# Four first up units in the banks of the down product, and down products 0 and 1 both behind round 3

## The chip, the core and the metric

The kernel is one program for one core of a Trainium2 chip. The core has a matrix engine (TensorE, PE), a vector engine (VectorE, DVE), a scalar engine (ScalarE, ACT), a general one (GpSimd, POOL) and a queue that here issues nearly all loads (SyncE, SP). Each engine works through its own list of instructions in order and waits on semaphores that the others raise. The metric is the time of the whole program on the device in microseconds (us), the median of several runs.

## What is computed

Two transformer-like blocks follow each other on 256 tokens of width 1024, in float32. The part that the change touches is the feed-forward net (FFN) of the first block, of width 2816:

```python
def conv_ffn(h, w_up, taps, conv_b, w_down, rows):
    a, g = jnp.split(h @ w_up, 2, axis=-1)
    bsz, t, f = g.shape
    ...
        g2, tp = g.reshape(bsz, rows, GRID_W, f), taps
    gc = lax.conv_general_dilated(g2, tp[:, :, None, :].astype(g.dtype), (1, 1), 'SAME',
                                  dimension_numbers=('NHWC', 'HWIO', 'NHWC'), feature_group_count=f)
    gc = gc.reshape(bsz, t, f) + conv_b
    return (a * jax.nn.gelu(gc, approximate=False)) @ w_down
...
        h2 = modulate(rmsnorm(x, norm_ffn[l]), sh2, sc2)
        x = x + g2 * conv_ffn(h2, w_up[l], conv_w[l], conv_b[l], w_down[l], rows)
```

The factor `g2` ahead of the product is one of six vectors of `silu(c) @ w_ada`; its four blocks of weights (ada20 to ada23) are still worked off during this FFN.

## The kernel before

**Weights.** All weights come from HBM in chunks of 1 MB, in the one order of the list `CHUNKS`. SP loads chunk n into place n % 3 of the ring `raw` (`RING = 3`, load at L510) as soon as chunk n-3 has been used up: a product chunk when DVE has split it (semaphore `w_lo`), an ada chunk when DVE has folded it (`ada_late`). A product chunk is split in two halves of the value: ACT writes the high part `whi` (`split_hi`, L595), DVE the low part `wlo` (`split_lo`, L604); both have three places as well, and a place is free when PE has done the product three chunks (ada ones not counted) earlier (`multiplied`). Every product is then three matmuls (L1140 to L1142): high by high, high by low, low by high.

**The FFN in rounds.** `for j in range(FFT // 2)` runs 11 rounds on each engine. Round j has two up products, `fg{j}` (the branch that is convolved) and `fa{j}` (the other), each of 48 matmuls into one PSUM bank, and a down product `fd{j}`, also of 48 matmuls, which adds into banks 4 to 7 over all rounds. On PE a round is `gemm(fg{j})`, `gemm(fa{j})` and, from round 2 on, `down(j - 2)` (L1484 to L1490). The up units lie in banks 0 and 1 in turn (all fg in one, all fa in the other) and wait until the unit two earlier is emptied; one exception was there already: fa1 goes to bank 6, and fa2 then waits for fa0.

ACT in round j: copies fg{j} out of its bank in four steps (L834, L835), splits two chunks (whi), waits for the convolution, gelu (L848), from round 2 on a third split, then `uhi`, the high part of the round's result (L854). DVE in round j: four of the eight outer taps for both halves (L2191, 8 instructions), a split (wlo), the other four taps, a split, the product with fa{j} (L2205), from round 2 on a third split, then `ulo` (L2212). The chunk that is split is always the third after the one just multiplied. In rounds 1, 3, 5 and 7 an ada chunk is worked on as well: ACT scales it in two halves (L823), DVE folds it at the end of the round (L2218 to L2220), and this frees its place in `raw`.

What sets the order around the change is written out by hand: the list of chunks (`ffn_chunks`, `ADA_AT`), the lists of the three engines and the banks in `g_bank` and `g_open`. Around it, the order of chunks before is fg2, ada20, fa2, fd0, fg3, fa3, fd1, fg4, ada21, fa4, fd2, fg5.

## Time and profile before

| | us |
|---|---|
| median of 3 runs | 1023.29 |
| lowest, highest run | 1022.83, 1025.29 |
| the profiled execution | 1022.01 |
| its span, first to last instruction | 1020.2 |
| PE busy in the span | 964.4 (95%) |
| DVE busy, ACT busy | 744.3 (73%), 501.6 (49%) |

The trace is of one execution; times in it count from the start of the span. The rounds of the FFN run from about 237 to 441 us. In the rows, a duration includes the tail of an instruction that the next one already overlaps, so the step from one start to the next is the better measure of what an instruction takes in a row. "issue" marks idle time for which the profile finds no releaser.

### The profile page before, as it was taken

How to read it: one execution, taken by the hardware profiler on the slowest of the kernel's cores; microseconds unless marked ns; L12 is line 12 of the kernel's file. 1: busy time of each engine (PE TensorE's matmuls, PEld its weight loads, DVE VectorE, ACT ScalarE, POOL GpSimd, SP SyncE). 2: the span in 40 equal slices, each digit the busy share in tenths (PEclk: the TensorE clock that was granted, in tenths of full speed). 3: DMA queues.
4: the chain of work that ended last, by engine and by line, in shares of the span. 5: the costliest groups of instructions: out<-in, count | busy, mean ns of one | idle time of the engine just before them, and what ended most of it. 6: DMA issues, size and time to landing. Idle time of an engine off the chain costs nothing.

```text
span 1020.2 us, 17808 instructions
## 1 busy us (share of the span) xinstructions
PE 964.4 (95%) x7576; PEld 904.6 (89%) x7576; DVE 744.3 (73%) x1083; ACT 501.6 (49%) x623; POOL 16.7 (2%) x35
## 2 busy tenths in 40 slices
PE   5999999899989999989998989989999999999997
PEld 3578999898989999988997989989989999999986
DVE  5879988878888798847977966644595776666664
ACT  5644344625464464427754544324543554545463
POOL 0000000002000000000100000000000000000000
PEclk9999999999989999979999999999999999999999
DMA  9997353364366557654756875735653455555541
GB/s 339 284 294 257 115 166 125 124 207 143 114 226 214 193 173 247 174 116 83 145 122 152 139 151 172 123 97 118 143 180 129 145 192 180 195 178 195 176 165 42
DMA packets 142719, 171.76 MB, mean 168 GB/s; under 512 B 3241, under 2 KB 129473, under 8 KB 142641
## 3 DMA queue, kind: packets, MB, share of 16 engines
q1 hardware_dynamic: 140352, 165.63, 55.7%
q0 software_dynamic: 1088, 2.57, 0.7%
q10 hardware_dynamic: 1200, 2.43, 0.7%
q8 instruction: 60, 0.98, 0.4%
q14 instruction: 19, 0.15, 0.0%
HBM read 169.55 MB, written 1.06 MB: 167 GB/s over the span
## 4 chain that ended last, share of the span: by engine, by line
PE 59%; DVE 10%; ACT 4%; issue 3%; DMA 2%; DVEq 0%; ACTq 0%
PE bank L1140 18%; PE bank L1142 17%; PE bank L1141 17%; DVE wlo L604 3%; ACT whi L595 2%; PE bank L1678 2%; DMA raw<-in_w_in_dram 1%; DVE arena L2326 1%; DVE arena L2191 1%; PE bank L1619 1%; DVE arena L2287 1%; DVE arena L1865 1%; DMA raw<-in_w_up_dram 1%; ACT arena L953 0%; PE bank L1455 0%
## 5 line engine op out<-in xcount | busy, mean ns | idle before, releaser
L1140 PE MATMUL bank<-hhi,whi 128*128 128x256 f32 (+1 forms) x1744 | 512.6, 294 | 23.7 <-issue 8.0
L1141 PE MATMUL bank<-hlo,whi 128*128 128x256 f32 (+1 forms) x1744 | 505.4, 290 | 0.0
L1142 PE MATMUL bank<-hhi,wlo 128*128 128x256 f32 (+1 forms) x1744 | 505.3, 290 | 0.0
L604 DVE TENSOR_TENSOR wlo<-raw,whi 128x2048 fp32r<-128x2048 f32 x131 | 299.7, 2290 | 151.2 <-ACT whi L595 110.7
L1140 PEld LDWEIGHTS bank<-hhi,whi 128*128 128x128 f32 x1744 | 339.7, 195 | 33.2 <-issue 21.1
L1141 PEld LDWEIGHTS bank<-hlo,whi 128*128 128x128 f32 x1744 | 340.0, 195 | 4.1 <-issue 1.2
L1142 PEld LDWEIGHTS bank<-hhi,wlo 128*128 128x128 f32 x1744 | 339.6, 195 | 2.5
L595 ACT ACTIVATE whi<-raw 128x2048 fp32r<-128x2048 f32 x131 | 250.5, 1912 | 119.6 <-PE bank L1142 69.1
L1140 PE MATMUL bank<-whi,hhi 128*128 128x256 f32 (+1 forms) x256 | 88.2, 344 | 0.8 <-ACT arena L1102 0.8
L1141 PE MATMUL bank<-wlo,hhi 128*128 128x256 f32 (+1 forms) x256 | 86.7, 339 | 0.0
L1142 PE MATMUL bank<-whi,hlo 128*128 128x256 f32 (+1 forms) x256 | 86.6, 338 | 0.0
L2191 DVE SCALAR_TENSOR_TENSOR arena<-arena,params 128x256 f32<-128x256 f32 x176 | 71.6, 479 | 6.5 <-ACT arena L835 6.5
L2581 DVE SCALAR_TENSOR_TENSOR arena<-bank,params,arena 128x255 f32<-128x255 f32 (+1 forms) x88 | 36.4, 476 | 31.5 <-ACT arena L1050 31.2
L1140 PEld LDWEIGHTS bank<-whi,hhi 128*128 128x128 f32 x256 | 49.2, 192 | 6.7 <-ACT arena L1102 1.2
L1142 PEld LDWEIGHTS bank<-whi,hlo 128*128 128x128 f32 x256 | 49.2, 192 | 5.1
L1141 PEld LDWEIGHTS bank<-wlo,hhi 128*128 128x128 f32 x256 | 49.3, 193 | 4.8 <-issue 0.2
L946 ACT ACTIVATE arena<-bank 128x512 f32<-128x512 f32 x18 | 10.8, 598 | 77.0 <-PE bank L1142 77.0
L1050 ACT ACTIVATE arena<-bank,params 128x256 f32<-128x256 f32 x44 | 18.5, 470 | 61.1 <-PE bank L1142 61.1
L806 ACT ACTIVATE arena<-XT 128x512 f32<-128x512 f32 x12 | 7.6, 631 | 44.9 <-DVE XT L2155 28.3
L1956 DVE SCALAR_TENSOR_TENSOR raw<-raw,small 128x256 f32<-128x256 f32 x72 | 29.5, 478 | 0.0
L1678 PE MATMUL bank<-arena 64*64 64x64 f32 x512 | 18.6, 220 | 2.9 <-issue 2.9
L1678 PEld LDWEIGHTS bank<-arena 64*64 64x64 f32 x512 | 16.9, 135 | 4.6 <-issue 3.0
(351 smaller groups left out, 866.9 us busy)
## 6 DMA issues: line engine op xcount, KB each, us to landing
raw<-in_w_in_dram SPq DMA_DIRECT2D x46, 1024.0 KB, 8.4
raw<-in_w_up_dram SPq DMA_DIRECT2D x44, 1024.0 KB, 5.1
raw<-in_w_down_dram SPq DMA_DIRECT2D x22, 1024.0 KB, 5.0
raw<-in_w_ada_dram SPq DMA_DIRECT2D x19, 1024.0 KB, 5.3
raw<-in_w_branch_dram SPq DMA_DIRECT2D x6, 1024.0 KB, 5.4
arena<-in_w_ada_dram SPq DMA_DIRECT2D x10, 512.0 KB, 9.3
raw<-in_w_out_dram SPq DMA_DIRECT2D x4, 1024.0 KB, 5.0
raw<-in_w_o_dram SPq DMA_DIRECT2D x4, 1024.0 KB, 5.1
```

The lines of the kernel that those rows point to most:

```text
L595: act.activation(whi[:, g % RING, :], raw[:, n % RING, :], ACT.Copy).then_inc(w_hi, 1)
L604: dve.tensor_tensor(wlo[:, g % RING, :], raw[:, n % RING, :], whi[:, g % RING, :].bitcast(F32), ALU.subtract).then_inc(w_lo, 1)
L946: act.activation(dst, two(g_bank(u)), func).then_inc(g_empty["act"], 1)
L1050: ins = act.activation(acc2[:, b, n, t, :], g_bank(f"s{w}{j}")[:, T * t:T * (t + 1)], ACT.Copy, scale=col)
L1140: pe.matmul(o, wh, ah, start=start, stop=False, **kw)
L1141: pe.matmul(o, wh, al, start=False, stop=False, **kw)
L1142: return pe.matmul(o, wl, ah, start=False, stop=stop, **kw)
L1619: ins = pe.matmul(o[:, P * h:P * (h + 1)], lhsT(c, h), rhs(c, h), start=True, stop=True)
L1678: ins = pe.matmul(o[m, 64 * h:64 * h + 64], lhsT[k, 4 * c + h, m] if lhsT is ANT else lhsT[k, 4 * c + h, :], rhs[k, 4 * c + h, :], start=T ...
L1956: ins = dve.scalar_tensor_tensor(out=w[:, k % 2, :], in0=w[:, k, :], scalar=silu_c[:, k, 0:1], in1=w[:, k % 2, :], op0=ALU.mult, op1=ALU.add)
L2191: ins = dve.scalar_tensor_tensor(out=a, in0=pad[:, b, t, dy:dy + 4, dx:dx + 64], scalar=par("conv_w", k=FFT * tap + 2 * j + t), in1=a, op0 ...
L2581: ins = dve.scalar_tensor_tensor(out=acc2[:, b, n, t, d:T], in0=ps[:, T * t:T * (t + 1) - d], scalar=par("ffn_conv", k=2 * FFT * (2 - d) + ...
```

## The change

The order of loads, the banks and the order of work in rounds 2 and 3 change together. The lines that only drop a condition which is always true are left out of the diff.

- `downs(tag, j)` says which down products follow round j: none after round 2, both 0 and 1 after round 3, the others as before. The list of chunks, the PE's list and the splits on ACT and DVE use it. The order of chunks becomes fg2, ada20, fa2, fg3, fa3, fd0, fd1, fg4, ada21, fa4, fd2, fg5.
- fg1, fa1, fg2, fa2 go to banks 4 to 7, which the down product doesn't use until down 0, and wait for no bank. fg3 and fa3 wait for fg0 and fa0, the last users of their banks. PE waits ahead of down 0 until fg2 and fa2 are emptied.
- Round 2 has two splits on ACT and DVE instead of three, round 3 has four instead of three. On ACT the first half of ada21's scaling moves behind the second split of round 3.

```diff
+    def downs(tag, j):
+        if tag == "f" and j in (2, 3):
+            return [(), (0, 1)][j - 2]
+        return (j - 2,) if j > 1 else ()
...
-            if j > 1:
-                chunk(f"{tag}d{j - 2}", rows(down, 2 * (j - 2)), (2, D))
+            for d in downs(tag, j):
+                chunk(f"{tag}d{d}", rows(down, 2 * d), (2, D))
...
+        FILL_BANK = {"fg1": 4, "fa1": 5, "fg2": 6, "fa2": 7}
+        FILL_AFTER = {"fg1": None, "fa1": None, "fg2": None, "fa2": None, "fg3": "fg0", "fa3": "fa0"}
...
-            return bank[6] if u == "fa1" else bank[g_banks[g_no(u) % 2]]
+            return bank[FILL_BANK.get(u, g_banks[g_no(u) % 2])]
...
-                if j + 1 in ADA_AT:
+                if j + 1 in ADA_AT and j != 3:
                     ada_scale(ADA_AT[j + 1], 0)
...
+                if j == 3:
+                    ada_scale(ADA_AT[j + 1], 0)
+                for d in downs("f", j)[:-1]:
+                    split_hi(act, G[f"fd{d}"] + RING)
...
-                if j > 1:
-                    split_hi(act, G[f"fd{j - 2}"] + RING)
+                for d in downs("f", j)[-1:]:
+                    split_hi(act, G[f"fd{d}"] + RING)
...
-                before = {"fa1": None, "fa2": g_no("fa0")}.get(u, n - 2)
-                if n >= 2 and before is not None:
-                    e, k = g_emptied(before)
+                if u in FILL_AFTER:
+                    if FILL_AFTER[u]:
+                        pe.wait_ge(*g_done(FILL_AFTER[u]))
+                elif n >= 2:
+                    e, k = g_emptied(n - 2)
                     pe.wait_ge(g_empty[e], k)
...
-                if j == 2:
-                    pe.wait_ge(*g_done("fa1"))
-                if j > 1:
-                    down(j - 2)
+                if j == 3:
+                    pe.wait_ge(*g_done("fg2"))
+                    pe.wait_ge(*g_done("fa2"))
+                for d in downs("f", j):
+                    down(d)
...
+                for d in downs("f", j)[:-1]:
+                    split_lo(dve, G[f"fd{d}"] + RING)
...
-                if j > 1:
-                    split_lo(dve, G[f"fd{j - 2}"] + RING)
+                for d in downs("f", j)[-1:]:
+                    split_lo(dve, G[f"fd{d}"] + RING)
```

Where it moves instructions, the first place is the load queue between the load of fg2 and that of fg5. Before, from the load of fg2 on (w_up is an fg or fa chunk, w_down an fd chunk, w_ada an ada chunk; the wait is for the chunk three earlier):

```order
43 L510 DMA raw<-in_w_up_dram 128x8x256 [waits w_lo] x2
44 L510 DMA raw<-in_w_ada_dram 128x8x256 [waits w_lo]
45 L510 DMA raw<-in_w_up_dram 128x8x256 [waits w_lo]
46 L510 DMA raw<-in_w_down_dram 128x2x1024 [waits w_lo]
47 L510 DMA raw<-in_w_up_dram 128x8x256 [waits ada_late]
48 L510 DMA raw<-in_w_up_dram 128x8x256 [waits w_lo]
49 L510 DMA raw<-in_w_down_dram 128x2x1024 [waits w_lo]
50 L510 DMA raw<-in_w_up_dram 128x8x256 [waits w_lo]
```

And the same place after the change:

```order
43 L519 DMA raw<-in_w_up_dram 128x8x256 [waits w_lo] x2
44 L519 DMA raw<-in_w_ada_dram 128x8x256 [waits w_lo]
45 L519 DMA raw<-in_w_up_dram 128x8x256 [waits w_lo] x2
46 L519 DMA raw<-in_w_up_dram 128x8x256 [waits ada_late]
47 L519 DMA raw<-in_w_down_dram 128x2x1024 [waits w_lo] x2
48 L519 DMA raw<-in_w_up_dram 128x8x256 [waits w_lo]
```

The load that waits for the fold of ada20 was that of fg3 and is now that of fa3; the two w_down loads stand together behind it.

The second place is DVE's list in round 3, from its first taps to the fold of ada21. Before (the three wlo are those of fg4, fa4 and fd2):

```order
261 L2191 SCALAR_TENSOR_TENSOR arena<-arena,params 128x256 [waits dve_step] x6
262 L604 TENSOR_TENSOR wlo<-raw,whi 128x2048 [waits g_full,w_hi,raw_loaded2]
263 L2191 SCALAR_TENSOR_TENSOR arena<-arena,params 128x256 [waits dve_step] x8
264 L604 TENSOR_TENSOR wlo<-raw,whi 128x2048 [waits g_full,w_hi,raw_loaded1]
265 L2205 TENSOR_TENSOR arena<-bank,arena 128x512 [waits g_full,u_hi,gelu_out]
266 L604 TENSOR_TENSOR wlo<-raw,whi 128x2048 [waits down_used,w_hi,raw_loaded2]
267 L2212 TENSOR_TENSOR hlo<-arena,hhi 128x512 [waits down_used,u_hi]
268 L2218 TENSOR_TENSOR raw<-raw 128x1024 [waits ada_scaled]
```

After the change (the four wlo are those of fd1, fg4, fa4 and fd2):

```order
260 L2205 SCALAR_TENSOR_TENSOR arena<-arena,params 128x256 [waits dve_step] x6
261 L613 TENSOR_TENSOR wlo<-raw,whi 128x2048 [waits g_full,w_hi,raw_loaded1]
262 L2205 SCALAR_TENSOR_TENSOR arena<-arena,params 128x256 [waits dve_step] x8
263 L613 TENSOR_TENSOR wlo<-raw,whi 128x2048 [waits g_full,w_hi,raw_loaded2]
264 L613 TENSOR_TENSOR wlo<-raw,whi 128x2048 [waits down_used,w_hi,raw_loaded1]
265 L2220 TENSOR_TENSOR arena<-bank,arena 128x512 [waits g_full,u_hi,gelu_out]
266 L613 TENSOR_TENSOR wlo<-raw,whi 128x2048 [waits down_used,w_hi,raw_loaded2]
267 L2227 TENSOR_TENSOR hlo<-arena,hhi 128x512 [waits down_used,u_hi]
268 L2233 TENSOR_TENSOR raw<-raw 128x1024 [waits ada_scaled]
```

The split of fd1 has come in ahead of fg4's, which moved from between the two halves of the taps to behind them; the split of fa4 now waits for a down product.

## Rows read from the trace of the kernel before

**Rows 1.** The page: span, and busy time of each engine.
```profile
span 1020.2 us, 17808 instructions
PE 964.4 (95%) x7576; PEld 904.6 (89%) x7576; DVE 744.3 (73%) x1083; ACT 501.6 (49%) x623; POOL 16.7 (2%) x35
```

**Rows 2.** PE's waits: line, releaser, us in total, times, longest.
```profile
PE bank L1140 <- issue: 8.0, 4, 5.8
```

**Rows 3.** PE's timeline: start, us, engine, line, instruction, [idle before <- releaser].
```profile
284.15 0.55 PE L1140 MATMUL bank<-hhi,whi 128*128 128x256 f32 x1 [5.78 <-issue]
...
321.32 0.36 PE L1140 MATMUL bank<-hhi,whi 128*128 128x256 f32 x1 [0.46 <-issue]
...
357.19 0.36 PE L1140 MATMUL bank<-hhi,whi 128*128 128x256 f32 x1 [0.84 <-issue]
```

**Rows 4.** The chain that ended last, in time: start, us, what.
```profile
274.57 5.17 DMA raw<-in_w_up_dram
279.76 1.92 ACT whi L595
281.68 2.47 issue
...
284.71 0.21 PE bank L1141
...
289.42 0.12 PE bank L1142
```

**Rows 5.** The load queue's timeline: start and us of the issue.
```profile
274.57 1.00 SPq L510 DMA_DIRECT2D raw<-in_w_up_dram  x2
...
299.27 0.37 SPq L510 DMA_DIRECT2D raw<-in_w_down_dram  x1
311.31 0.99 SPq L510 DMA_DIRECT2D raw<-in_w_up_dram  x2
```

**Rows 6.** DVE's timeline, rounds 2 to 4.
```profile
289.94 2.28 DVE L604 TENSOR_TENSOR wlo<-raw,whi 128x2048 fp32r<-128x2048 f32 x1
...
293.79 3.25 DVE L2191 SCALAR_TENSOR_TENSOR arena<-arena,params 128x256 f32<-128x256 f32 x8 [0.96 <-ACT arena L835]
296.96 2.29 DVE L604 TENSOR_TENSOR wlo<-raw,whi 128x2048 fp32r<-128x2048 f32 x1
299.16 3.26 DVE L2191 SCALAR_TENSOR_TENSOR arena<-arena,params 128x256 f32<-128x256 f32 x8
302.32 2.29 DVE L604 TENSOR_TENSOR wlo<-raw,whi 128x2048 fp32r<-128x2048 f32 x1
...
306.07 2.29 DVE L604 TENSOR_TENSOR wlo<-raw,whi 128x2048 fp32r<-128x2048 f32 x1 [0.85 <-issue]
...
310.86 0.42 DVE L2220 TENSOR_TENSOR arena<-raw 128x256 f32<-128x256 f32 x1
...
318.93 2.29 DVE L604 TENSOR_TENSOR wlo<-raw,whi 128x2048 fp32r<-128x2048 f32 x1 [4.48 <-issue]
```

**Rows 7.** ACT's timeline, rounds 2 and 3.
```profile
290.06 0.63 ACT L854 ACTIVATE hhi<-arena 128x512 fp32r<-128x512 f32 x1 [0.37 <-DVE arena L2205]
292.18 0.39 ACT L834 ACTIVATE arena<-bank 128x256 f32<-128x256 f32 x1 [1.49 <-PE bank L1142]
...
304.06 1.92 ACT L595 ACTIVATE whi<-raw 128x2048 fp32r<-128x2048 f32 x1 [0.98 <-DMA raw<-in_w_down_dram]
```

**Rows 8.** Stretches behind waits: busy times, then PEclk; and two matmuls that end one.
```profile
284.20:288.30 4.10, 4.10 (x19) 4.10 (x20) 4.10 (x9) 1.52 (x3) 0.00 (x0) 0.50 0.83 269
201.40:204.40 3.00, 3.00 (x26) 3.00 (x27) 2.90 (x7) 1.26 (x2) 0.00 (x0) 1.00 0.00 0
482.60:485.60 3.00, 3.00 (x18) 3.00 (x17) 2.93 (x4) 2.99 (x5) 0.00 (x0) 0.58 0.04 9
...
482.33 0.36 PE L1140 MATMUL bank<-hhi,whi 128*128 128x256 f32 x1 [2.07 <-DVE arena L2287]
201.30 0.36 PE L1140 MATMUL bank<-hhi,whi 128*128 128x256 f32 x1 [2.72 <-ACT whi L595]
```

More of the change, by code:

```diff
@@ L838, in _ @@
                 ins.then_inc(g_empty["act"], 1)
-                if G[f"fg{j}"] + RING < N_SPLIT:
-                    split_hi(act, G[f"fg{j}"] + RING)
-                if j + 1 in ADA_AT:
+                split_hi(act, G[f"fg{j}"] + RING)
+                if j + 1 in ADA_AT and j != 3:
                     ada_scale(ADA_AT[j + 1], 0)
-                if G[f"fa{j}"] + RING < N_SPLIT:
-                    split_hi(act, G[f"fa{j}"] + RING)
+                split_hi(act, G[f"fa{j}"] + RING)
+                if j == 3:
+                    ada_scale(ADA_AT[j + 1], 0)
+                for d in downs("f", j)[:-1]:
+                    split_hi(act, G[f"fd{d}"] + RING)
                 if j + 1 in ADA_AT:
@@ L2198, in _ @@
                 ins.then_inc(conv_out, 1)
-                if G[f"fa{j}"] + RING < N_SPLIT:
-                    split_lo(dve, G[f"fa{j}"] + RING)
+                split_lo(dve, G[f"fa{j}"] + RING)
+                for d in downs("f", j)[:-1]:
+                    split_lo(dve, G[f"fd{d}"] + RING)
                 dve.wait_ge(gelu_out, j + 1)
```

## The prediction, made before the changed kernel ran

> **What bounds the kernel now.** I read four views in this order. First the page: TensorE (PE) is busy for 95% of the span [rows 1], so only time in which PE stands still can be won, and any new standstill is a loss. Second, the waits of PE: the largest sum is 8.0 us in 4 waits, the longest 5.8 us [rows 2]. PE's timeline places all four inside the first feed-forward part: 5.78 us before the matmul at 284.15, then 0.46, 0.84 and 0.90 us before those at 321.32, 357.19 and 393.13, of which three stand in [rows 3]. By their order these are the first matmuls of fg3, fg5, fg7 and fg9. Third, the chain of work shows what the long wait was for [rows 4]: a load of w_up issued at 274.57 lands 5.17 us later, ScalarE (ACT) makes whi for 1.92 us, VectorE (DVE) makes wlo in the 2.47 us called issue, PE goes on at 284.15. Fourth, the load queue: the load at 274.57 was issued right after DVE had folded ada20, since ada20 held the ring place that this load needs [rows 5]. So PE doesn't wait for a bank here; it waits for a place in the raw ring.
>
> From PE's next wait I read the same loop: fold of ada21 ends at 310.86 + 0.42 = 311.28, loads go out at 311.31, wlo of fg5 runs from 318.93 to 321.22, PE starts at 321.32 [rows 3, 5, 6]. PE was ready at 320.86. The slack of this loop is therefore below zero by 0.46 us: whatever delays the fold of ada21 delays PE by as much.
>
> **The change, part by part.**
>
> *Banks.* PE's first standstill in the rounds is the one before 284.15 [rows 2, 3]; up to the end of fa2 it never waits for a bank, so four units in other banks remove nothing there. For fg3 the bank wait falls away as well, but in the old order its weights were last, not its bank. Price 0, covered by the weights that come later.
>
> *The first standstill.* The new order of chunks is fg2, ada20, fa2, fg3, fa3, fd0, fd1. Loads look three chunks back: now fg3 takes the place of fg2 (early) and fa3 takes that of ada20. ACT and DVE in round 1 have the same number of splits as before, one of them of fg3 in place of fd0, so ada20 is folded at the same time and the load goes out at 274.57 again, now for fa3. PE does fg3 where it did down 0: both are 48 matmuls, 0.12 us apart [rows 4], 5.76 us. It comes to the end of fg3 at 278.4 and waits until 284.15 for fa3. Same work done, same wait, same slow matmuls behind it: 0 us.
>
> *Round 3 on DVE.* Here the sum is made. DVE splits in round 2 only two chunks (fa3, fd0) where it had three; the split at 289.94 [rows 6] goes. So ACT writes uhi at 290.06 as before [rows 7], can copy fg3 out straight after it (fg3 is long finished), 0.6 us later by the 0.63 of that row, and DVE starts 1.6 us behind the first of the four copies (292.18 to 293.79). The taps of round 3 start at about 290.06 + 0.6 + 1.6 = 292.2 and not at 293.79 [rows 6]: 1.6 us early.
> Against that stands the place of fg4's split. It was the first of the round: taps from 293.79, wlo from 296.96 to 299.25, and at 299.27 the load of fd2 went out into its ring place [rows 5, 6]. Now the first split is fd1's and fg4's comes after the second half of the taps: one wlo (299.16 - 296.96 = 2.20) and eight taps (302.32 - 299.16 = 3.17 by the start of the next row) later, 5.4 us. fg4's split then ends at 292.2 + 3.17 + 2.20 + 3.17 + 2.29 = 303.0, and the load of fd2 goes out 3.8 us later than before.
> From there to the fold I take the old distance: load at 299.27, whi at 304.06 which waited 0.98 us for that load, wlo at 306.07, ulo, fold to 311.28 [rows 5 to 7], 12.0 us. Nothing new comes between: wlo of fa4, whose load goes out when fd1 is split at 297.6 and lands at about 302.8 (5.2 after, as in [rows 4]), ends at about 307.1, ahead of the 307.8 at which fd2 lands; and down 1, for which fd2's place in whi must wait, ends at 303.6 as before. So ada21 is folded at 315.0, fg5's weights are ready 3.8 us later, and PE starts fg5 at about 325.1. PE itself has done the same six units by 320.9, so this standstill grows from 0.46 to 4.2 us. **Term: +3.8 us.**
>
> Bounds of it. Above: the whole 5.4 us, if ACT's early copy brings nothing. Below: 5.4 - 1.6 - 0.8 = 3.0, if DVE's 0.85 us of idleness before 306.07 [rows 6] takes up part; I take 3.8, because in the new order that idleness grows (DVE is free at 307.7 and waits for fd2 till 309.8) and hides nothing.
>
> *The clock.* After the 5.78 us wait, the stretch from 284.20 has a granted clock of 0.50, the 1.2 GHz level, and 19 matmuls in 4.1 us. After a wait of 2.07 us before 482.33 the stretch behind shows 0.58; after one of 2.72 us before 201.30 it shows 1.00 [rows 8]. A new wait of 4.2 us lies between them and I expect a fall: 15 matmuls at 0.213 instead of 0.12 us (the steps at 1.2 GHz and at the full level), 1.4 us. Of this PE gets back what it waits before fg7 anyway, 0.84 us [rows 3], as the loads of the next rounds hang on DVE and hardly on PE. **Term: +0.5 us**, from 0 (no fall) to 1.4 (nothing given back).
> By the Trainium skill (TensorE: Matmul & The Clock Gate, Loop structure matters more than you think) a wait for a DMA between matmuls lets PE go cold, whereas a copy out of PSUM does not; the trace agrees for the wait at 284.15, and 1.4 us would be the price here too.
>
> *Smaller things.* The new waits of PE before down 0 (banks of fg2 and fa2 emptied) are met at 290.0, when DVE has multiplied fa2; PE comes there at 292.1: 0. Behind that wait stand down 0 and down 1. Margins get thin: fd1's split ends at 297.7, PE wants it at 297.9; fg4's ends at 303.0, PE wants it at 303.6. Price 0, to 0.5 us if I err by half a microsecond. The end of round 3 moves scaling of ada21 on ACT behind one split; both halves end before 306.5, no one waits.
>
> *After fg5.* From there order and work are the old ones. Both old idle times (0.84, 0.90) stay, since DVE, ACT and loads form a loop of their own. The rest of the span is PE's: the shift of the FFN's end goes to the end.
>
> **Sum** against the profiled execution: 1022.01 + 3.8 + 0.5 = 1026.3 (its span 1020.2 would be 1024.5). That execution is 1.3 us below the median of 1023.29; on the median's scale the forecast is 1027.5 us, with own bounds of 1023.29 + 3.0 = 1026.3 and 1023.29 + 5.4 + 0.5 = 1029.2.
>
> **Rivals.**
> *B, the bank was the limit (faster).* Were the wait before 284.15 one for a bank, the fill would close it: -5.8 us and -1.8 for the 19 or 20 slow matmuls, less what the loads then still hold back: 1023.3 - 7.6 = 1015.7 us. It decides from the moment that fa3's weights are there before 278.4. For it speaks only that the trace names no releaser (issue) at 284.15. Against it: the chain through load, whi and wlo ends 0.1 us before the matmul [rows 4, 6]. In this case I give it 0.06.
> The Trainium skill (Perfetto Trace Analysis, Optimizing Tensor Performance, Matmuls) says that matmul groups should rotate through different PSUM banks so that one's copy out overlaps the next's matmuls; that is this rival, and the trace speaks against it in this stretch, as the load is what comes last.
> *C, part is given back (same).* If the loads after fg5 were paced by PE, the waits of 0.84 and 0.90 us would vanish once PE is late: 4.3 - 1.7 = 2.6, 1025.9 us; the same reading holds if DVE gains a little more than 1.6 us in round 3. Against it: DVE's rows from 318.93 on follow each other without PE in between. 0.20.
> *D, the thin margins break (slower still).* PE waits also for fd1's and fg4's splits and the full clock loss stays: +5.4 + 1.4 = +6.8, less nothing: 1030.1 us. It decides if wlo of fd1 ends later than 297.9. 0.12.
> *A, as forecast*: 0.62.
>
> **How the numbers follow.** A measurement of this kernel tells about 0.3% (3.1 us) from no change. Slower by more: D and nearly nine tenths of A, 0.12 + 0.55 = 0.67. Within: C and the rest of A, 0.27. Faster: B, 0.06. The range takes in A, C and most of D and leaves room below C, where the two terms of round 3 would cancel further: 1023.4 to 1029.8 us.
>
> **What would show it.** In the new profile: PE's wait of 5.8 us again, but before fa3, at about 284.1; DVE's taps of round 3 at about 292.2; the load of fd2 issued at about 303.0; the fold of ada21 ending at about 315; PE's wait before fg5 of about 4.2 us with a granted clock near 0.5 after it; later waits of 0.3 to 0.9 us as before. Wrong I would be if the first wait is gone or much shorter (B), or if the wait before fg5 is under 2 us.

## The result, and the profile after

The changed kernel took 1028.5 us (median of 7 runs, 1025.8 to 1031.4) where the kernel before, run beside it, took 1022.8 us (7 runs, 1016.0 to 1025.3). The ratio of the means of the two sets is 1.0069, with an interval of 1.0038 to 1.0100: slower, by 7.1 us of 1022.8 (the medians alone are 5.7 us apart). On the scale of the 1023.29 us before, that is 1030.3 us, just above the top of the range I gave (1029.8), and 2.8 us above the forecast. The interval reaches into the range, so the miss of the range by itself is thin; that the loss is larger than forecast is shown below by the traces and by a second set of runs. The sign was right, the size too small.

The page of the changed kernel, which answers to [rows 1]:

```profile
span 1026.7 us, 17809 instructions
PE 959.8 (93%) x7576; PEld 899.4 (88%) x7576; DVE 744.7 (73%) x1083; ACT 501.2 (49%) x623; POOL 16.7 (2%) x35
```

No matmul came or went (7576 in both). PE's busy time is 4.6 us less than before; that says little, since the same kernel was busy for 965.7 us in its second trace (e1). What can be compared are the waits. PE's timeline of the changed kernel, with the four waits that answer to [rows 3] (start, us, idle before it and what released it):

```profile
285.72 0.55 PE L1153 MATMUL bank<-hhi,whi 128*128 128x256 f32 x1 [5.73 <-issue]
...
329.10 0.55 PE L1153 MATMUL bank<-hhi,whi 128*128 128x256 f32 x1 [6.22 <-issue]
...
365.63 0.36 PE L1153 MATMUL bank<-hhi,whi 128*128 128x256 f32 x1 [0.44 <-issue]
...
401.51 0.36 PE L1153 MATMUL bank<-hhi,whi 128*128 128x256 f32 x1 [0.83 <-issue]
```

The line numbers are 9 to 15 higher than before: L1153 is the old L1140, L613 the old L604, L519 the old L510. The waits stand before fa3, fg5, fg7 and fg9. The first is as long as it was (5.73 against 5.78 us), only a unit later. The second has grown from 0.46 to 6.22 us. Together they are 13.2 us, where they were 8.0 [rows 2]: +5.2 us.

**One offset first.** The first matmul of fg0 starts at 239.15 us in this trace and at 237.55 in that of before, in code that the change doesn't touch. PE's granted clock shows it; the same stretch of both kernels, first after, then before (PE busy time and matmuls, PEld, DVE, ACT, POOL, then PEclk):

```profile
204.00:211.00 7.00, 7.00 (x54) 7.00 (x54) 2.32 (x2) 0.00 (x0) 0.00 (x0) 0.87 0.46 150
```

```profile
204.00:211.00 7.00, 7.00 (x61) 7.00 (x60) 3.05 (x4) 0.00 (x0) 0.00 (x0) 1.00 0.46 149
```

A granted clock of 0.87 leaves 54 matmuls in 7 us, one of 1.00 leaves 61. In e1, which is the changed kernel once more, the clock of that stretch was full, so the fall belongs to the execution, not to the change. Below I therefore measure from the first matmul of fg0. To where PE starts on the sums behind the first FFN it is 204.2 us before and 210.9 us after: **+6.8 us**. What follows the FFN is within 2 us of before (576.6 against 578.5 us). So the loss lies in the FFN, as forecast.

**Where it arises.** The loads of the changed kernel answer to [rows 5]:

```profile
304.60 0.37 SPq L519 DMA_DIRECT2D raw<-in_w_down_dram  x1
317.89 0.99 SPq L519 DMA_DIRECT2D raw<-in_w_up_dram  x2
```

and DVE's timeline to [rows 6]:

```profile
293.74 3.25 DVE L2205 SCALAR_TENSOR_TENSOR arena<-arena,params 128x256 f32<-128x256 f32 x8 [0.76 <-ACT arena L844]
296.92 2.28 DVE L613 TENSOR_TENSOR wlo<-raw,whi 128x2048 fp32r<-128x2048 f32 x1
299.12 3.25 DVE L2205 SCALAR_TENSOR_TENSOR arena<-arena,params 128x256 f32<-128x256 f32 x8
302.29 2.28 DVE L613 TENSOR_TENSOR wlo<-raw,whi 128x2048 fp32r<-128x2048 f32 x1
...
312.65 2.29 DVE L613 TENSOR_TENSOR wlo<-raw,whi 128x2048 fp32r<-128x2048 f32 x1 [3.35 <-issue]
...
317.44 0.42 DVE L2235 TENSOR_TENSOR arena<-raw 128x256 f32<-128x256 f32 x1
...
326.71 2.29 DVE L613 TENSOR_TENSOR wlo<-raw,whi 128x2048 fp32r<-128x2048 f32 x1 [5.68 <-issue]
```

The taps of round 3 start at 293.74 (forecast 292.2, with the offset of 1.6: 293.8). fg4's split, now behind the second half of the taps, starts at 302.29, and the load of fd2 goes out at 304.60 (forecast 303.0 + 1.6 = 304.6). Up to here the forecast holds to a tenth. Then two steps are longer than the same steps before. ACT's timeline of the changed kernel has the moments at which the two loads are used:

```profile
310.64 1.92 ACT L604 ACTIVATE whi<-raw 128x2048 fp32r<-128x2048 f32 x1 [2.20 <-DMA raw<-in_w_down_dram]
324.71 1.91 ACT L604 ACTIVATE whi<-raw 128x2048 fp32r<-128x2048 f32 x1 [10.19 <-DMA raw<-in_w_up_dram]
```

From issue to use, fd2's load takes 310.64 - 304.60 = 6.04 us (before: 304.06 - 299.27 = 4.79), and that of fg5 324.71 - 317.89 = 6.82 us (before: 5.61). Each is 1.2 us longer, and both lie on the loop that ends in fg5's weights. fg5 thus comes 329.10 - 239.15 = 89.95 us after fg0, 6.2 us later than before (321.32 - 237.55 = 83.77), where I had 3.8. The stretch behind fg5 brings the other 0.6 us.

**What differs in the two loads.** In the profile's list of DMA queues there is, besides the queue of the loads, one called "instruction", which now and then moves a single packet of 0.02 MB. The DMA page of two windows of half a microsecond in the changed kernel, 306.0 to 306.5 and 321.0 to 321.5, one in either load (queue, packets, MB, share of the 16 engines):

```profile
q8 instruction: 1, 0.02, 13.1%
```

```profile
q1 hardware_dynamic: 187, 0.19, 107.5%
q8 instruction: 1, 0.02, 13.7%
```

Before, no such packet lay in fg5's load. The same view of that kernel, 311.3 to 317 (the last line gives both loads issued then, and the median to landing):

```profile
q1 hardware_dynamic: 1470, 1.49, 80.1%
issues: line engine op xcount, KB each, median us to landing
raw<-in_w_up_dram SPq DMA_DIRECT2D x2, 1024.0 KB, 6.9
```

But one lay in another load of that kernel, that of fg4, issued at 284.08. Two windows of its DMA view, 284 to 285 and 286.5 to 287.5, have the time from issue to landing and the packet:

```profile
raw<-in_w_up_dram SPq DMA_DIRECT2D x1, 1024.0 KB, 6.5
```

```profile
q8 instruction: 1, 0.02, 6.7%
```

Whether these packets lengthen the loads, or only lie there, is what e7 and e9 ask.

### The profile page after: what moved, and what is told of

The parts are those of the page before. It is cut to its first block, busy times and chain, and to the rows that moved or that the text cites. A ratio compares the mean times of both kernels' runs of the same rounds, so it can differ in the third digit from the quotient of the medians.

```text
span 1026.7 us, 17809 instructions
## 1 busy us (share of the span) xinstructions
PE 959.8 (93%) x7576; PEld 899.4 (88%) x7576; DVE 744.7 (73%) x1083; ACT 501.2 (49%) x623; POOL 16.7 (2%) x35
## 4 chain that ended last, share of the span: by engine, by line
PE 53%; DVE 13%; ACT 4%; issue 4%; DMA 4%; DVEq 0%; ACTq 0%
PE bank L1153 16%; PE bank L1154 16%; PE bank L1155 16%; DVE wlo L613 4%; DVE arena L2205 2%; PE bank L1692 2%; DMA raw<-in_w_in_dram 2%; ACT whi L604 2%; DMA raw<-in_w_up_dram 1%; DVE arena L2341 1%; DVE arena L2302 1%; DVE arena L2371 1%; DMA raw<-in_w_down_dram 1%; DVE arena L1879 1%; PE bank L1633 1%
## 5 line engine op out<-in xcount | busy, mean ns | idle before, releaser
L1153 PE MATMUL bank<-hhi,whi 128*128 128x256 f32 (+1 forms) x1744 | 512.3, 294 | 30.0 <-issue 13.6
L613 DVE TENSOR_TENSOR wlo<-raw,whi 128x2048 fp32r<-128x2048 f32 x131 | 299.8, 2290 | 154.4 <-ACT whi L604 107.5
L1153 PEld LDWEIGHTS bank<-hhi,whi 128*128 128x128 f32 x1744 | 339.2, 195 | 39.4 <-issue 27.3
L604 ACT ACTIVATE whi<-raw 128x2048 fp32r<-128x2048 f32 x131 | 250.4, 1912 | 130.9 <-PE bank L1155 68.5
L1153 PE MATMUL bank<-whi,hhi 128*128 128x256 f32 (+1 forms) x256 | 87.9, 344 | 0.8 <-ACT arena L1113 0.8
L1153 PEld LDWEIGHTS bank<-whi,hhi 128*128 128x128 f32 x256 | 49.0, 191 | 6.7 <-ACT arena L1113 1.2
```

Of the source, the lines that this page charges most:

```text
L604: act.activation(whi[:, g % RING, :], raw[:, n % RING, :], ACT.Copy).then_inc(w_hi, 1)
L613: dve.tensor_tensor(wlo[:, g % RING, :], raw[:, n % RING, :], whi[:, g % RING, :].bitcast(F32), ALU.subtract).then_inc(w_lo, 1)
L1153: pe.matmul(o, wh, ah, start=start, stop=False, **kw)
```

## The experiments

All ratios are against the kernel before, run on the same chip in the same call; its medians there were 1021.3, 1021.4, 1022.1 and 1021.0 us. The number that I compare beside the time is the length of the FFN in each trace, from fg0's first matmul to the sums behind it: 204.2 us before, 210.9 us after. A load is timed in two ways: to its use, as above, and to its landing, the moment when all of it has arrived, which can be earlier when ACT is still busy.

### The change again, and its parts

**e1** is the changed kernel, with nothing edited.

> The changed kernel once more, to see which parts of its loss come back. In its first trace PE waited 5.73 us before fa3 and 6.22 us before fg5, the load of fd2 took 6.0 us from issue to use and that of fg5 6.8 us (4.8 and 5.6 in the trace of the kernel before), and PE was already 1.6 us late at the first round. Theory 1 (the place of fg4's split on VectorE makes the loop longer by 3.8 us, the slower loads and the 1.6 us are chance): wait before fg5 between 4.0 and 6.5 us, loads between 4.8 and 6.8 us, the 1.6 us gone or back as the clock falls; time 4 to 7 us above the kernel before. Theory 2 (the new order of loads makes these two loads slower each time): both loads again 6.0 and 6.8 us, wait before fg5 again 6.2 us.

Measured: 1028.8 us (1026.9 to 1032.2), ratio 1.0077 (1.0052 to 1.0102); FFN 211.6 us. PE's timeline has 5.75 us before fa3 and, before fg5:

```profile
328.00 0.55 PE L1153 MATMUL bank<-hhi,whi 128*128 128x256 f32 x1 [6.42 <-issue]
```

The two loads took 5.80 and 6.95 us, again with an instruction packet in each. So neither the 6.2 us nor the longer loads were chance. The clock behind fg5's wait was at 0.50 here, where the first trace had 0.66, and from fg5 on this trace loses 1.4 us, not 0.6.

**e5** keeps the changed order of the work but takes the banks of before, so that PE has to wait for them:

```
-        FILL_BANK = {"fg1": 4, "fa1": 5, "fg2": 6, "fa2": 7}
-        FILL_AFTER = {"fg1": None, "fa1": None, "fg2": None, "fa2": None, "fg3": "fg0", "fa3": "fa0"}
+        FILL_BANK = {"fa1": 6}
+        FILL_AFTER = {"fa1": None, "fa2": "fa0"}
```

> The changed kernel with the banks and bank waits of the kernel before; order of loads, splits and PE's units stay as changed. Now fa3 must wait until fa2 is emptied, so PE's wait before fa3 should grow from 5.7 to about 11.5 us. Theory 1 (behind round 3 the loop of loads and splits sets the time, not PE): the wait before fg5 shrinks by the same 5.8 us to about 0.5, later parts and the time stay within 1.5 us of the changed kernel. Rival (PE sets the time there): the 5.8 us add up, 5 to 6 us slower than the changed kernel.

Measured: 1026.4 us, ratio 1.0060 (1.0039 to 1.0080); FFN 210.3 us. One of the ten executions took 5215 us and isn't in the ratio. By the ratios this is 1.7 us below e1, a little over the 1.5 us expected, and within the intervals. PE's timeline:

```profile
290.71 0.56 PE L1153 MATMUL bank<-hhi,whi 128*128 128x256 f32 x1 [11.02 <-DVE arena L2220]
...
328.20 0.36 PE L1153 MATMUL bank<-hhi,whi 128*128 128x256 f32 x1 [0.37 <-issue]
```

PE waits 11.02 us for a bank before fa3 and comes out 6 us later than with the new banks (290.71, in e1 284.72), and yet fg5 starts at the same time (328.20, in e1 328.00) and the FFN is no longer. The changed order makes the loss with the old banks too.

It would be too much to read from this that PE's place in the rounds doesn't matter, for two things cancel. PE's lateness does reach the loop: ACT's splits in round 3 now wait for PE. ACT's timeline has the split of fd2, 2.2 us behind the landing of its load:

```profile
310.65 1.92 ACT L604 ACTIVATE whi<-raw 128x2048 fp32r<-128x2048 f32 x1 [1.73 <-PE bank L1155]
```

Against that both loads are short: fd2's lands after 4.91 us and fg5's after 5.88, where the two traces of the changed kernel have 6.02 and 5.78, and 6.80 and 6.93. PE's instructions come later here, and no instruction packet lies in either load.

**e6** does the other part alone: the order of before, with fg1 and fa1 in the banks 4 and 5.

```
-            return bank[6] if u == "fa1" else bank[g_banks[g_no(u) % 2]]
+            return bank[{"fg1": 4, "fa1": 5}.get(u, g_banks[g_no(u) % 2])]
...
-                before = {"fa1": None, "fa2": g_no("fa0")}.get(u, n - 2)
+                before = {"fg1": None, "fa1": None, "fg2": g_no("fg0"), "fa2": g_no("fa0")}.get(u, n - 2)
```

> The kernel before with fg1 and fa1 in banks 4 and 5 and no bank wait for fg1, fa1; fg2 and fa2 wait for fg0 and fa0. Orders unchanged. Theory 1: no unit waited for its bank there, so PE's waits are 5.8, 0.5, 0.8 and 0.9 us as before and the time is within 0.2% of the kernel before. Rival (banks cost something in the first rounds): 1 to 3 us faster and a shorter wait before fg3.

Measured: 1020.6 us, ratio 1.000 (0.998 to 1.002); FFN 203.5 us, and PE still waits 5.76 us in the first place. Banks alone bring nothing and cost nothing.

**e2** gives round 3 of the changed kernel the three splits that it had before, of fg4 and fa4 in the old places and of fd2 last, and has fd1 split in round 2:

```
+                up3 = ("fg4", "fa4") if j == 3 else (None, None)
+                split_hi(act, G[up3[0]] if up3[0] else G[f"fg{j}"] + RING)
...
-                for d in downs("f", j)[-1:]:
-                    split_hi(act, G[f"fd{d}"] + RING)
+                if j > 1:
+                    split_hi(act, G[{2: "fd1", 3: "fd2"}[j]] if j < 4 else G[f"fd{j - 2}"] + RING)
```

and the same on DVE. The first half of ada21's scaling goes back to its old place too.

> The changed kernel, but with the split of fd1 back in round 2 on ScalarE and VectorE, so that rounds 2 and 3 have three splits each and fg4's split stands between the two halves of the taps again; banks, order of loads and order on PE stay as changed. Theory 1 (the split's place on VectorE is the loss): the load of fd2 goes out 4 to 5 us earlier against the first round, PE waits under 1 us before fg5, time 4 to 7 us below the changed kernel and within 2 us of the kernel before. Theory 2 (order and speed of loads are the loss): the wait before fg5 shrinks by at most 3.8 us and 2.4 us of it stay; time 2 us or more above the kernel before. In both the wait of 5.7 us before fa3 stays, as it hangs on the fold of ada20.

Measured: 1017.3 us (1015.2 to 1021.5), ratio 0.9960 (0.9943 to 0.9977); FFN 203.4 us. In its trace the load of fd2 goes out at 299.32, the fold of ada21 ends at 312.4, fg5's load takes 5.30 us, and PE has no wait before fg5. So it is the place of the splits, fg4's behind the taps above all, that the loss hangs on: with it undone, the whole 6.8 us and a little more are gone, although the banks, the two down products together and the order of the weights on PE are the changed kernel's. This run doesn't tell the parts of the loss from each other, as both loads are short here too (to landing 4.74 and 5.27 us). It is 11.5 us below e1, where I expected 4 to 7. The time is below that of before by 4 us, of which the FFN shows 0.8 and the part behind it 2.0 in the one trace; I can't place more of it.

### What the loop is worth

If the ring place behind a fold is what holds PE up, an earlier fold must shorten both waits. **e3** is the kernel before, with the fold of the ada chunk (three additions) moved from the end of the round to right behind the second half of the taps:

```
                 ins.then_inc(conv_out, 1)
+                if j + 1 in ADA_AT:
+                    c = ADA_AT[j + 1]
+                    dve.wait_ge(ada_scaled, 2 * (c - 19))
+                    w = raw[:, ada_place[c] % RING, :].rearrange("p (k n) -> p k n", k=KT)
...
+                    dve.tensor_tensor(acc_late[:, c % 4, :], w[:, 0, :], w[:, 1, :], ALU.add).then_inc(ada_late, 1)
```

> The kernel before with one edit: VectorE folds the ada chunk right behind the second half of the taps instead of at the end of the round, so its ring place comes free 4 to 6 us earlier. If PE's long wait is for a ring place (my reading): the wait of 5.8 us before fg3 shrinks to about 2 us, those before fg5, fg7 and fg9 vanish, fewer slow matmuls; 5 to 8 us faster than before. If it is for a bank or for the load path itself: wait and time unchanged.

Measured: 1012.1 us (1009.7 to 1014.7), ratio 0.9909 (0.9885 to 0.9933); FFN 195.6 us, 8.6 less than before. Its load queue and PE (two views):

```profile
271.46 0.99 SPq L510 DMA_DIRECT2D raw<-in_w_up_dram  x2
```

```profile
274.30 0.39 PE L1140 MATMUL bank<-hhi,whi 128*128 128x256 f32 x1 [0.58 <-DVE arena L2212]
...
281.96 0.35 PE L1140 MATMUL bank<-hhi,whi 128*128 128x256 f32 x1 [1.65 <-ACT whi L595]
```

The load that stood at 274.57 [rows 5] goes out 3.1 us earlier, 4.2 us when both are counted from fg0 (at 238.65 here). The gain is a little more than the 5 to 8 us expected. PE's waits in the FFN come to 2.2 us, where they were 8.0, and the three later ones are gone; since PE now waits 1.65 us and not 5.78, its clock also stays at the full level behind it (1.00 from 281.96 to 285), where before it was at 0.50 [rows 8].

**e4** puts both together, the early fold and the changed kernel with the three splits of e2.

> The changed kernel with three splits each in rounds 2 and 3 and with the early fold. If the new order has a gain that only the ring hid, it is faster than the kernel before with the early fold by what PE still waits there; by the ring theory both orders do the same work ahead of the same load, so the two come out within 1 us of each other, 5 to 8 us faster than the kernel before, with a wait of about 2.5 us before fa3.

Measured: 1012.3 us (1008.9 to 1014.4), ratio 0.9908 (0.9883 to 0.9934); FFN 196.8 us. PE's timeline, and two stretches behind the wait:

```profile
283.31 0.36 PE L1150 MATMUL bank<-hhi,whi 128*128 128x256 f32 x1 [2.23 <-ACT whi L604]
```

```profile
283.40:286.40 3.00, 3.00 (x19) 3.00 (x20) 3.00 (x9) 0.00 (x0) 0.00 (x0) 0.70 0.69 223
286.40:289.00 2.60, 2.60 (x18) 2.60 (x17) 2.60 (x2) 2.44 (x2) 0.00 (x0) 0.69 0.45 149
```

Once the fold is early, the new banks and the new order add nothing to it: e3 and e4 are the same within their intervals. PE waits 2.23 us in one place, and behind that its granted clock is 0.70.

**e8 and e10** fill that wait of e4 with idle products (they go into a free bank and are overwritten), to ask what the clock costs: 14 products in e8, 4 in e10.

```
+                if j == 3:
+                    pe.wait_ge(*g_done("fg1"))
+                    keep_clock(bank[4], 4)
                 gemm(f"fa{j}", T)
```

> The kernel of e4 (changed order, three splits in rounds 2 and 3, early fold) with 14 idle matmuls of 256 columns in the wait of 2.2 us before fa3; their results are never read. In e4's trace the clock fell to 0.70 behind that wait. If the fall comes from PE standing still, the clock stays at 1.00, fa3 and down 0 save about 2 us, and the time is 1 to 2.5 us below e4's 1012.3. If the splits set the pace there, the time stays.

> The kernel of e4 with 4 idle products (8 matmuls of 0.22 us, 1.8 us) in the wait of 2.2 us before fa3. In e8 14 of them took 6.2 us and held fa3 up by 4 us, which ate the gain. Now PE should wait about 0.4 us, the clock should stay at 1.00 behind, where e4 had 0.70, and the end of the FFN should come 2 us earlier against its first round than in e4 (196.8 us from the first matmul of fg0 to the last sums). Time 1 to 2 us below e4's 1012.3; that is near what these runs can tell.

Measured: e8 1010.1 us (1007.5 to 1014.0), ratio 0.9899 (0.9870 to 0.9928); e10 **1007.4 us** (1005.6 to 1010.9), ratio 0.9868 (0.9841 to 0.9895), the fastest kernel of the study. In e8 the idle products were too many:

```profile
279.58 6.21 PE L1189 MATMUL bank<-cf 128*128 128x256 f32 x28
```

They ran for 6.21 us and held fa3 up: the FFN is 198.9 us, 2.1 longer than in e4. That e8 is faster all the same is not the clock's doing; it comes from the late standstill that e12 is about. In e10 they fit:

```profile
281.02 1.89 PE L1189 MATMUL bank<-cf 128*128 128x256 f32 x8
283.41 0.36 PE L1150 MATMUL bank<-hhi,whi 128*128 128x256 f32 x1 [0.50 <-issue]
```

and the granted clock behind them is 1.00. The FFN of e10 is 195.5 us, 1.3 less than in e4, where I expected 2. The other 3.6 us of its gain lie far behind, as the last experiments show.

### The term that was too small

**e11** is the changed kernel with 12 idle products in PE's wait before fg5, to have the clock's share of the loss:

```
+                    if j == 5:
+                        keep_clock(m_bank("A5"), 12)
```

> The changed kernel with 12 idle products (24 matmuls, 5.4 us) on PE in its wait before fg5; their results are never read. My term for the clock: the fall behind that wait costs 1.4 to 1.9 us on the spot, of which the wait before fg7 gives back what it can. So with the clock held at 1.00 fg5 starts at the same time, ends 1.5 us earlier, and the wait before fg7 grows from 0 to 0.4 us to about 1 us; the FFN ends 0.5 to 1 us earlier. If the fall costs its full price, the FFN ends 1.5 to 1.9 us earlier.

Measured, one run: 1025.4 us; FFN 210.4 us, which is 0.5 less than in the changed kernel and 1.2 less than in e1. PE's timeline and the stretch behind:

```profile
330.23 0.35 PE L1153 MATMUL bank<-hhi,whi 128*128 128x256 f32 x1 [1.42 <-issue]
```

```profile
330.00:333.00 3.00, 2.77 (x23) 2.80 (x24) 3.00 (x9) 0.73 (x1) 0.00 (x0) 1.00 0.56 174
```

The clock is full, fg5 starts no earlier (90.2 us after fg0, in the changed kernel 89.95), and PE gives part of it back before fg7, where it waits 0.86 us (0.44 in the changed kernel). By this single run the clock is worth 0.5 to 1.2 us in this place. Its loads took 6.20 and 6.84 us, with a packet in each: a third trace of that.

**e7 and e9** ask whether the instruction packets make the two loads long. If they carry PE's instructions, more instructions on PE ahead of that place move them to an earlier time. Both are the changed kernel with products of one column in the wait before fa3, into a bank that is free there; 48 in e7, 16 in e9:

```
+                if j == 3:
+                    pe.wait_ge(*g_done("fg1"))
+                    for n in range(16):
+                        pe.matmul(bank[4][:, n:n + 1], ident, ones[:, 0:1], start=True, stop=True)
```

> The changed kernel with 48 one-column matmuls on PE in its wait before fa3, which is 5.7 us long anyway; their results are never read. They move PE's later instructions by 48 matmuls and 48 weight loads, and with them the moments at which its instructions are fetched from memory. In both traces of the changed kernel such a fetch falls into the loads of fd2 and of fg5, which take 5.8 to 6.9 us from issue to use; without one the like loads take 4.8 to 5.2. Theory 3 (the fetch within a load makes it longer): with the fetches moved out, fd2's load takes about 4.8 and fg5's about 5.4 us, the wait before fg5 shrinks from 6.3 to about 4 us, time 2 to 2.5 us below the changed kernel. Rival (these loads are slow for another reason, such as their place in the queue): both stay at 5.8 to 6.9 us and the time too.

Measured: 1027.4 us, ratio 1.0059 (1.0036 to 1.0082). The products cost more than I had allowed for:

```profile
279.60 16.57 PE L1502 MATMUL bank<-cf 128*128 128x1 f32 x96
```

Each ran as two matmuls, of 0.17 us on average, and they held PE up by 10 us. The time says nothing, therefore. The trace does: the packet had moved to 318.1, ahead of fg5's load, and that load took 5.28 us. No packet lay in fd2's load either, which landed after 4.91 us.

The 0.17 us are a mean of two levels. The clock fell while PE ran these products without a pause (PE busy time and matmuls, then the other engines, then PEclk):

```profile
279.60:283.00 3.40, 3.40 (x34) 3.40 (x32) 0.00 (x0) 1.91 (x1) 0.00 (x0) 1.00 1.05 398
...
286.00:290.00 4.00, 4.00 (x20) 4.00 (x21) 4.00 (x8) 0.63 (x1) 0.00 (x0) 0.50 0.82 268
```

At the full level one takes 0.10 us, at 0.50 it takes 0.20.

> The changed kernel with 16 one-column float32 products on PE in its wait before fa3; their results are never read. In e7 48 such products came as 96 matmuls of 0.17 us and held PE up by 10 us; 16 should take 5.5 us and fit into the wait of 5.7. They move the later fetches of PE's instructions earlier by 32 matmuls and 32 weight loads, near 4 us: from 1 to 3 us behind the issue of the loads of fd2 and fg5 to before it. Theory 3 (a fetch within a load makes it longer): fd2's load takes 4.8 to 5.0 us to use, fg5's 5.2 to 5.9, the wait before fg5 shrinks from 6.3 to 4 us, time 2 to 2.5 us below the changed kernel. Rival: loads stay at 5.8 to 6.0 and 6.8 to 7.0 us, and so do wait and time.

Measured: 1020.7 us (1016.0 to 1025.5), ratio 0.9987 (0.9965 to 1.0009). The 16 products took 3.63 us of a wait of 5.97, and PE was not held up by them. PE's timeline and the load queue:

```profile
326.22 0.55 PE L1153 MATMUL bank<-hhi,whi 128*128 128x256 f32 x1 [4.12 <-issue]
```

```profile
303.96 0.37 SPq L519 DMA_DIRECT2D raw<-in_w_down_dram  x1
316.38 0.99 SPq L519 DMA_DIRECT2D raw<-in_w_up_dram  x2
```

The packets start at 299.7 and 315.2, out of both loads. fd2's load is used 5.18 us after its issue at most, fg5's 5.45 us; fg5 starts 326.22 - 238.43 = 87.8 us after fg0, which is 4.0 us later than before. Without the two packets the wait is 4.1 us, as the prediction had it (4.2). And the load that a packet now does lie in, that of fa4 (issued at 298.59), took 6.61 us, where it took 5.17 in the changed kernel. The lengthening went where the packet went.

The other traces bear this out. For three loads in each of the 14 traces, from issue to landing:

| load of | a packet starts inside, over 3 us before the landing | none, or only in the last microsecond |
|---|---|---|
| fg4 | 6.5 to 7.2 us, 9 traces | 5.0 to 5.4 us, 5 traces |
| fd2 | 5.8 to 6.2 us, 4 traces | 4.7 to 5.0 us, 10 traces |
| fg5 | 6.8 to 6.9 us, 3 traces | 5.1 to 5.9 us, 11 traces |

In six of the ten short loads of fd2 (before, e2, e3, e4, e6, e8) a packet does start inside, 0.2 to 0.9 us before the landing. So late it costs nothing.

Yet the FFN is only 0.9 us shorter than in the changed kernel (210.0 us): behind this wait the clock stood at 0.50 for the whole of a 4.2-us stretch with 20 matmuls (in the changed kernel 0.66, 25 matmuls). It had been at 0.50 before that too, behind the 2.34 us that PE still stood before fa3, after the one-column products. Most of the 8 us between e9 and the changed kernel (7.4 between the spans of the two traces) must lie elsewhere. The largest part, 3.9 us, lies around the small matmuls of the inversion, in code that no edit here touches; about 2 us I can't place. PE's timeline there, of the kernel before:

```profile
661.43 1.61 PE L1678 MATMUL bank<-arena 64*64 64x64 f32 x47
665.93 0.69 PE L1678 MATMUL bank<-arena 64*64 64x64 f32 x17 [2.89 <-issue]
```

of the changed kernel:

```profile
667.14 1.61 PE L1692 MATMUL bank<-arena 64*64 64x64 f32 x47
672.47 0.73 PE L1692 MATMUL bank<-arena 64*64 64x64 f32 x17 [3.72 <-issue]
```

and of e9:

```profile
666.64 2.08 PE L1696 MATMUL bank<-arena 64*64 64x64 f32 x64
```

In both kernels PE stands still for 2.9 and 3.7 us between the 47th and the 48th of 64 equal matmuls, with nothing to wait for that the profile shows, and there is an instruction packet in that gap (663.5 to 664 us in the kernel before). In e9 the 64 run through.

**e12** puts the same 16 products into the kernel before, in its wait before fg3, to ask whether this gain is the change's or can be had by either:

> The kernel before with the same 16 one-column products as e9, here in PE's wait of 5.8 us before fg3; their results are never read. e9 came out 8 us below the changed kernel, though its FFN was only 1 to 2 us shorter; the rest stood in the matrix inversion, where PE stood still for 2.9 us between two of 64 small matmuls in the kernel before (3.4 to 3.7 us in the changed one), with an instruction packet in that time and slow matmuls after it, and did not in e7 to e11, all of which have more PE instructions. Theory (this standstill hangs on the number of PE instructions ahead and not on the change): it is gone here too, the kernel is 4 to 6 us faster than before, and e9, its counterpart in the changed order, is 4 to 6 us slower than this one. If e9's gain came from the changed order: no gain here.

Measured: 1015.6 us (1013.8 to 1018.6), ratio 0.9951 (0.9933 to 0.9969), 5.4 us less than the kernel before; FFN 203.5 us, about as before.

```profile
661.02 2.08 PE L1682 MATMUL bank<-arena 64*64 64x64 f32 x64
```

The standstill is gone here too, and the stretch around it is 4.6 us shorter, of 6.6 us between the two spans. So e9 is to be compared with e12, not with the kernel before: 1020.7 - 1015.6 = 5.2 us slower, with the late standstill in neither. The two come from different calls; by their ratios it is 0.9987 - 0.9951, or 3.7 us. The loss by the changed order stays, at a little less than what the FFN shows (210.0 - 203.5 = 6.5 us).

## Why the prediction fell short

*What bounds the kernel: right.* PE didn't wait for a bank in the rounds. e6 gave it banks and nothing came of it. That e5's wait of 11 us for one cost nothing is weaker support, since shorter loads made up for it there. The first standstill came back one unit later, 5.73 us long (forecast 5.78). Rival B, 1015.7 us, is out.

*Round 3 on DVE, up to the load of fd2: right.* The step of 5.4 us less 1.6 us gives 3.8 us, and the trace has the load at 304.60, 65.45 us after fg0, where it was at 61.72: +3.7 us. e2, which puts the splits back, gets the whole loss back; e9, where the loads are as short as before, has fg5 4.0 us late.

*From there to fg5: the step that failed.* I wrote "From there to the fold I take the old distance ..., 12.0 us. Nothing new comes between", and took fg5's weights as equally far behind the fold. The path holds two loads, and each took 1.0 to 1.4 us more than the same load before, in all three traces of the changed kernel with nothing altered ahead of fg5 (its first, e1 and e11: 6.04 and 6.82 us, 5.80 and 6.95, 6.20 and 6.84, against 4.79 and 5.61). An instruction packet lay early in each; where e9 moved the packets out, the loads took 5.18 and 5.45 us. That makes the term 6.2 us and not 3.8. It was mis-sized because I took a duration of a load from one row and moved it 4 us, without looking at what else the DMA engines carried at the new time. The trace of the kernel before had the warning: fg4's load, with a packet in it, took 6.5 us. The range had no bound for it: its upper end was the 5.4 us that ACT's part could cost, with the loads fixed.

*The clock: right in kind, low by some tenths.* I had +0.5 us, from 0 to 1.4. From fg5 on the changed kernel loses 0.6 us in its first trace and 1.4 in e1, and e11 puts the clock's share at 0.5 to 1.2. The wait before fg7 fell from 0.84 to 0.44 us, that before fg9 hardly (0.90 to 0.83), so part was given back, as the text said, and not all. e9, with a wait of 4.1 us and the clock at 0.50 behind it, lost 210.0 - 204.2 - 4.0 = 1.8 us from fg5 on, more than my upper bound.

*The rivals.* C wanted the waits before fg7 and fg9 (1.74 us together) to vanish; 1.27 us of them stayed in the first trace and 0.83 in e1, so the small part that was given back didn't bring the time near C's. D had nearly the time that came (1030.1 against 1030.3 us), but not by its mechanism: its condition was that PE also waits for the splits of fd1 and fg4, and the trace has no such waits. That the time came out near D's is chance: a mechanism that was right and a duration that was not gave the size of another rival.

*The sum.* Of the 6.8 us in the FFN, 3.7 are the moved split, 2.5 the two longer loads and 0.6 the clock. The measured ratio says 7.1 us, with an interval of 3.9 to 10.2, and 6.8 lies in it; the parts behind the FFN (the late standstill is 0.8 us longer) can't be told from the spread of the runs.

*What stays open.* That the packets are PE's instructions is shown only by their moving when PE's instructions are added (e7, e9); the profile doesn't name who fetches. How 0.02 MB can make a load of 1 MB over a microsecond longer, and why only when it comes early, no run shows. And why e2 is 4 us faster than the kernel before is not explained.

## What to carry over

Ask for each wait of the bounding engine what its last releaser was itself waiting for, until a resource comes up; here it was a place in the raw ring behind a fold, three engines back. Banks that gave PE more room were worth nothing there (e6), while moving three small additions ahead of the last splits of the round was worth 9.2 us. And when a step is moved along the time axis, what lies beside it at the new time is part of its price: a load's duration is to be bounded by the slowest like it in the trace, not taken from the one row.

## What the runs showed of the hardware

**Instruction packets cost time in two ways.** The first is in the table of e9: a load of 1 MB landed about 1 to 2 us later when a packet started in it early, and no later when one started in its last microsecond. And among 64 matmuls of 64 columns PE stood for 1.9 to 3.7 us at the 48th, in each of the eight traces in which nothing had been added on PE ahead of it (a packet starts in that gap, in e4 and e6 0.4 us ahead of it); in the six others it didn't stand. In these, the runs in which 8 to 96 matmuls were added ahead (e7 to e12) the part of the program around this place, between two loads of ACT's tables, took 107.3 to 107.4 us, and without them 110.8 to 112.6 us. That is 3.4 to 5.3 us of 1020 which hang on how many instructions PE has run before, not on the code at the place.

By the Trainium skill (Runtime: NRT & Kernel Launch, Instruction fetch mechanics) an engine's instructions come in blocks of 16 KiB, fetched ahead by its own DMA queue, and crossing a block is mostly hidden, because instructions are given out more slowly than they are fetched. The size of the packets (0.02 MB) agrees with it; "mostly hidden" doesn't hold among small matmuls in this case, where the gap is 1.9 to 3.7 us.

**The clock behind a wait.** Behind 1.65 us of standing (e3) the granted clock stayed at 1.00; behind 2.23 us (e4) it was 0.70; behind 5.73 us (after) 0.50. One and the same wait of 2.72 us, in code that no edit touches, left it at 1.00 in the kernel before [rows 8], e1, e5, e6 and e9, and at 0.54 to 0.66 in the changed one, e2, e3, e7, e8 and e12. The row of the changed kernel in the same stretch:

```profile
201.40:204.40 3.00, 3.00 (x18) 3.00 (x19) 2.91 (x7) 1.26 (x2) 0.00 (x0) 0.66 0.00 0
```

So whether the clock falls behind a wait of this length differs from one execution to the next. In e10, where eight idle matmuls of 256 columns filled 1.89 us of such a wait, it stayed at 1.00. Products of one column didn't hold it: it fell to 0.50 while PE ran them in e7, and was at 0.50 behind a wait of 2.34 us that followed 3.63 us of them in e9.

**A product of one column isn't small.** 16 of them in float32 ran as 32 matmuls in 3.63 us, 0.11 us each at the full clock. The idle products of 256 columns, also in float32, ran as 28 matmuls in 6.21 us, 0.22 us each (e8), so one column costs half as much as 256. It costs nearly as much as one of the kernel's own matmuls of 256 columns on split values, 0.12 us.
